# First layer's output product on one set of split weights, its norm's gain and bias folded into the next modulation, and two changes beside it

## The reference

```python
def _layer_norm(x, g, b):
    ...
    return ((xf - mu) * lax.rsqrt(var + EPS) * g + b).astype(x.dtype)

def _post_norm(x, y, gate, g, b):
    return _layer_norm(ALPHA * x + gate * y, g, b)

# layer ab (i = 0)
            h = x * (1.0 + sc[:, None]) + sh[:, None]
            y = _ab_mixer(h, ab_w_in[j], ab_pool_w[j], ab_pool_scale[j], ab_sgu_w[j], ab_sgu_b[j], ab_w_out[j])
            ...
                yc = _ab_mixer(hc, ab_w_in[j], ab_pool_w[j], ab_pool_scale[j], ab_sgu_w[j], ab_sgu_b[j], ab_w_out[j])
                ctx = _post_norm(ctx, yc, cgt, ab_ln_g[j], ab_ln_b[j])
            x = _post_norm(x, y, gt[:, None], ab_ln_g[j], ab_ln_b[j])
# layer cd (i = 1)
            hc = ctx * (1.0 + csc) + csh
            ... _split_cd(hc @ cd_w_in[j])
            h = x * (1.0 + sc[:, None]) + sh[:, None]
            f_in, f_gate, cq, ckv, kr, d_gate = _split_cd(h @ cd_w_in[j])
```

## Time and profile before

| | us |
|---|---|
| median of three runs | 3071.2 |
| lowest, highest | 3066.11, 3073.33 |
| profiled execution | 3069.66 |
| its span in the trace | 3067.8 |
| PE busy | 2848.2 (93%) |
| DVE, ACT, POOL busy | 1177.4, 971.5, 173.5 |
| mean DMA share of 16 engines | 25.3% |

### The profile page before, as it was taken

How to read it: one execution, slowest core, us unless ns; L and a number is a source line. 1 busy time by engine, 2 the same in 40 slices (tenths; PEclk the granted TensorE clock), 3 DMA queues, 4 the chain that set the end, 5 groups by cost and what they waited for, 6 DMA issues and landing times.

```text
span 3067.8 us, 33482 instructions
## 1 busy us (share of the span) xinstructions
PE 2848.2 (93%) x14067; PEld 2288.3 (75%) x14067; DVE 1177.4 (38%) x1720; ACT 971.5 (32%) x1437; POOL 173.5 (6%) x289
## 2 busy tenths in 40 slices
PE   4998949999799999899799999999998998899998
PEld 3876738667688888677488888888887775688887
DVE  2133472245533324344643332433324444543322
ACT  2211232244232223444432222322224445332221
POOL 0130010000100000000110000000000000000000
PEclk7999779999899999899699999999998998799999
DMA  7432123100223323211023323223232111123321
GB/s 249 145 102 83 55 82 109 48 1 1 76 96 96 96 96 96 59 56 45 24 70 110 99 95 122 83 96 96 96 110 73 55 42 42 42 92 95 103 100 72
DMA packets 208908, 253.89 MB, mean 83 GB/s; under 512 B 6384, under 2 KB 187191, under 8 KB 208760
## 3 DMA queue, kind: packets, MB, share of 16 engines
q1 hardware_dynamic: 208760, 251.76, 25.3%
HBM read 249.64 MB, written 2.10 MB: 82 GB/s over the span
## 4 chain that ended last, share of the span: by engine, by line
PE 85%; DVE 7%; ACT 3%; issue 2%; POOL 1%; SPq 1%; DMA 1%; DVEq 0%; POOLq 0%; ACTq 0%
PE psum L740 82%; DVE w_lo L1786 1%; PE psum L1199 1%; PE psum L810 1%; ACT w_hi L1357 1%; PE psum L1124 1%; POOL stats_first L2350 1%; DVE stats_first L1861 0%; DVE work L1854 0%; DVE X L1857 0%; DMA mod_w<-in_ab_w_mod 0%; SPq L713 0%; DVE h_lo L1795 0%; DVE spare_lo L1786 0%; SPq L618 0%
## 5 line engine op out<-in xcount | busy, mean ns | idle before, releaser
L740 PE MATMUL psum<-h_hi,w_hi 128*128 128x512 f32 (+1 forms) x2096 | 788.5, 376 | 34.9 <-issue 15.1
L740 PE MATMUL psum<-h_lo,w_hi 128*128 128x512 f32 (+1 forms) x2096 | 780.0, 372 | 0.0
L740 PE MATMUL psum<-h_hi,w_lo 128*128 128x512 f32 (+1 forms) x2096 | 779.6, 372 | 0.0
L1786 DVE TENSOR_TENSOR w_lo<-raw,w_hi 128x2048 fp32r<-128x2048 f32 (+1 forms) x182 | 419.0, 2304 | 806.3 <-ACT w_hi L1357 805.9
L740 PEld LDWEIGHTS psum<-h_hi,w_hi 128*128 128x128 f32 x2096 | 399.1, 190 | 111.1 <-issue 29.3
L740 PEld LDWEIGHTS psum<-h_hi,w_lo 128*128 128x128 f32 x2096 | 398.6, 190 | 68.5
L740 PEld LDWEIGHTS psum<-h_lo,w_hi 128*128 128x128 f32 x2096 | 399.0, 190 | 67.0 <-issue 1.0
L1357 ACT ACTIVATE w_hi<-raw 128x2048 fp32r<-128x2048 f32 (+1 forms) x182 | 344.0, 1893 | 240.0 <-PE psum L740 235.7
L740 PE MATMUL psum<-w_hi,ff_hi 128*128 128x512 f32 x576 | 226.5, 393 | 0.0
L740 PE MATMUL psum<-w_lo,ff_hi 128*128 128x512 f32 x576 | 226.4, 393 | 0.0
L740 PE MATMUL psum<-w_hi,ff_lo 128*128 128x512 f32 x576 | 223.9, 389 | 0.0
(11 more groups left out here) (282 smaller groups left out, 3371.7 us busy)
## 6 DMA issues: line engine op xcount, KB each, us to landing
raw<-in_ffn_w_gate SPq DMA_DIRECT2D x44, 1024.0 KB, 5.3
raw<-in_ffn_w_up SPq DMA_DIRECT2D x44, 1024.0 KB, 5.3
raw<-in_ffn_w_down SPq DMA_DIRECT2D x44, 1024.0 KB, 4.9
raw<-in_w_in SPq DMA_DIRECT2D x36, 512.0 KB, 5.1
raw<-in_ab_w_in SPq DMA_DIRECT2D x10, 1024.0 KB, 5.7
mod_w<-in_ab_w_mod SPq DMA_DIRECT2D x8, 1024.0 KB, 10.6
raw<-in_ab_w_out SPq DMA_DIRECT2D x8, 1024.0 KB, 4.9
raw<-in_w_out SPq DMA_DIRECT2D x8, 1024.0 KB, 4.9
```

The costliest lines, as they stand in the source:

```text
L740: return pe.matmul(o, lhsT, rhs, start=start, stop=stop, skip_group_check=True)
L1786: dve.tensor_tensor(lo[:, 0:nk * n], raw[c % 2][:, 0:nk * n], hi[:, 0:nk * n].bitcast(F32), ALU.subtract).then_inc(*w_lo_made.mark(key))
```

## The change

1. One set of split weights `ab_out` (four chunks, of which 2 and 3 lie in `ab_spare`) serves X and context. ACT and DVE split chunk 1 between the pool and the sgu part, chunks 2 and 3 after the last sgu head. `AB_TAIL` gives the order of norms and turns on ACT, DVE and POOL.
2. PE does chunks 0 and 1 for all X tiles, then chunks 2 and 3 tile by tile with the turns of X two behind; context chunks 0 and 1; then before each context tile's chunks 2 and 3 a turn of X. Layer cd's chunk 0 waits for X alone; the context turns stand behind its halves, and chunk 5 waits for context.
3. The norm's gain and bias go into the scale and shift of the next modulation (four small DVE operations; two more small loads at the start). X itself is needed later as residual and gets gain and bias from POOL, eight operations behind all six deviations. The gate diagonals no longer wait for them; layer cd's norm does.
4. DVE adds `sgu_b` (loaded to all partitions) in one operation more per sgu result; PE's 24 one-row products go.
5. DVE's half of a modulation is four `tensor_scalar` operations from PSUM with scale and shift.
6. Each step of a value product becomes two, of 64 query columns, on PSUM partitions 0 to 63 and 64 to 127.
7. The mixing constants have four semaphores. `band_bias`, `far`, `strict`, `tri` are issued after PE's last output tile of the FFN, the distances after its norm, the others after the fourth chunk. DVE's sums stand at chunk 3, ACT's exponential at chunk 4, the rest at chunk 5.

```diff
-    for part in ("ab_x", "ab_c"):
-        for c in range(4):
-            add((part, c), "ab_w_out", 0, "rows", 256 * c, 2, True)
+    for c in range(4):
+        add(("ab_out", c), "ab_w_out", 0, "rows", 256 * c, 2, True)
...
-        scale_odd = sb(ab_tail, "one_plus_scale_odd", [P, KT, 2])
+        ab_spare = [(sb(ab_tail, "spare_hi", [P, 2048], F32R), sb(ab_tail, "spare_lo", [P, 2048], F32R)) for _ in range(2)]
...
-                        landed = consts_landed[layer]
...
+                        raws_to(begin + 3)
+                        sp.wait_ge(*psum_full["y", before, NT - 1])
+                        sp.dma_start(band_bias[:, :, :], A["l_band_bias"][layer].rearrange("h q k -> q h k")).then_inc(*band_landed.mark(layer))
+                        sp.dma_start(far[:, :], A["l_far_bias"][layer].partition_broadcast(P)).then_inc(*band_landed.mark(layer))
+                        sp.dma_start(strict[:, :, :], A["k_strict"].rearrange("s p n -> p s n")).then_inc(*stick_landed.mark(layer))
+                        sp.dma_start(tri[:, :], A["k_tri"]).then_inc(*stick_landed.mark(layer))
+                        sp.wait_ge(*residual["normed", before, NT - 1])
+                        sp.dma_start(dist, A["k_distance"]).then_inc(*dist_landed.mark(layer))
+                        raws_to(begin + 4)
+                        sp.dma_start(sub_g[:, :], A["diff_subln_g_2"][layer].partition_broadcast(P)).then_inc(*lam_landed.mark(layer))
+                        for i, name in enumerate(("q1", "k1", "q2", "k2")):
+                            sp.dma_start(lam[:, i, :], A[f"diff_lambda_{name}_2"][layer].partition_broadcast(P)).then_inc(*lam_landed.mark(layer))
                         raws_to(CHUNK[s, 3])
...
-                        mm(bank(b, P, q * P), v_norm[:, off // P + q, hd * P:(hd + 1) * P], sgu_wT[:, hd, :], True, False)
-                        m = mm(bank(b, P, q * P), ones[0:1, :], sgu_b[0:1, hd * P:(hd + 1) * P], False, True)
+                        m = mm(bank(b, P, q * P), v_norm[:, off // P + q, hd * P:(hd + 1) * P], sgu_wT[:, hd, :], True, True)
                     done(m, ("sgu", hd, r))
...
+            def out_part(s, c, i, off):
+
...
+                for h in range(2):
+                    b = 2 * i + h
+                    if c == 0:
+                        claim(b, ("y", s, i, h))
+                    for kk in range(2):
+                        k = 2 * c + kk
+                        if s == "ab_x":
+                            ab_ready(i, k, h)
+                        m = mm3(bank(b), tokens(h_hi, k, off, P), tokens(h_lo, k, off, P), w[0][:, kk, h * BANK:(h + 1) * BANK],
+                                w[1][:, kk, h * BANK:(h + 1) * BANK], k == 0, k == KT - 1)
+                return m
+
+            def x_turn(i):
+                pe.wait_ge(*normed["ab_x", i])
                 turn("xo", i, X[:, i, :], (2 * i, 2 * i + 1))
 
...
+            def c_turn(i):
+                pe.wait_ge(*normed["ab_c", i])
+                turn("ct", i, CTX[:, i, :])
+
...
+            for c in range(2):
+                begin(("ab_out", c))
+                for i in range(NT):
+                    m = out_part("ab_x", c, i, i * P)
+                done(m, ("chunk", "ab_x", c))
+            for i in range(NT):
+                for c in (2, 3):
+                    if i == 0:
+                        begin(("ab_out", c))
+                    m = out_part("ab_x", c, i, i * P)
+                done(m, ("y", "ab_x", i))
+                if i > 1:
+                    x_turn(i - 2)
+            for c in range(2):
+                for i in range(NC):
+                    m = out_part("ab_c", c, i, L + i * P)
+                done(m, ("chunk", "ab_c", c))
+                end(("ab_out", c))
+            for i in range(NC):
+                x_turn(2 + i)
+                for c in (2, 3):
+                    m = out_part("ab_c", c, i, L + i * P)
+                done(m, ("y", "ab_c", i))
+            for c in (2, 3):
+                end(("ab_out", c))
+            rot.at = 0
...
-            pe.wait_ge(*h_lo_made["ct", NC - 1, 1])
+            pe.wait_ge(*h_lo_made["xo", NT - 1, 1])
...
+                if ch == 5:
+                    pe.wait_ge(*h_lo_made["ct", NC - 1, 1])
...
+                    if ch == 0:
+                        c_turn(j)
                     if ch == 1:
                         gate_row(("gate_cd", j))
...
                     for k in range(6):
-                        m = mm(bank(b, 64), probsT[(n - 2) % 2][:, k * P:(k + 1) * P], v_all[:, k, hd * 64:(hd + 1) * 64], k == 0, k == 5)
+                        for p0 in (0, 64):
+                            m = mm(psum[p0:p0 + 64, b * BANK:b * BANK + 64], probsT[(n - 2) % 2][:, k * P + p0:k * P + p0 + 64],
+                                   v_all[:, k, hd * 64:(hd + 1) * 64], k == 0, k == 5)
...
+                if s == "ab_out":
+                    act.wait_ge(*h_lo_made["sgu", 3, 1])
...
             for kind in ("pool", "sgu"):
+                if kind == "sgu":
+                    split_at(CHUNK["ab_out", 1])
...
+            split_at(CHUNK["ab_out", 2])
+            split_at(CHUNK["ab_out", 3])
+            for step, s, i in AB_TAIL:
+                if (step, s, i) == ("norm", "ab_c", 1):
+                    split_at(CHUNK["cd_in", 1])
...
                     if ch < 2:
                         copy(f_in[:, g, :], event, full(event), cd_kept)
+                        if ch == 0:
+                            turn("ct", j, h_hi, L + j * P, scale_odd[:, :, 1], shift_odd[:, :, 1])
...
-                act.wait_ge(*lam_made["sums", s])
-                act.activation(lam_s[:, 2:4], lam_s[:, 0:2], ACT.Exp).then_inc(*lam_exp.mark(s))
...
+                        if step[1] == 4:
+                            act.wait_ge(*lam_made["sums", s])
+                            act.activation(lam_s[:, 2:4], lam_s[:, 0:2], ACT.Exp).then_inc(*lam_exp.mark(s))
...
+                for k in range(4):
+                    m = dve.tensor_scalar(wv[:, k, :], full(event, P, k * P), scale[:, 4 + k:5 + k], shift[:, 4 + k:5 + k], ALU.mult, ALU.add)
+                m.then_inc(*part_made.mark(("sum", event)))
+                freed[event] = part_made["sum", event]
...
+                if s == "cd":
+                    dve.wait_ge(*ln_made["ab_x", t])
...
+            split_at(CHUNK["ab_out", 1])
...
-                    dve.tensor_tensor(w, full(event, n), u_gated[:, hd, off:off + n], ALU.mult).then_inc(*part_made.mark(event))
-                    freed[event] = part_made[event]
+                    dve.tensor_tensor(w.rearrange("p (q i) -> p q i", i=P), full(event, n).rearrange("p (q i) -> p q i", i=P),
+                                      sgu_b[:, hd, :].unsqueeze(1).broadcast_to([P, n // P, P]), ALU.add).then_inc(*part_made.mark(("biased", event)))
+                    freed[event] = part_made["biased", event]
+                    dve.wait_ge(*part_made["biased", event])
+                    dve.tensor_tensor(w, w, u_gated[:, hd, off:off + n], ALU.mult).then_inc(*part_made.mark(event))
                     split_lo_of(event, tokens(h_lo, 4 + hd, off, n), w, tokens(h_hi, 4 + hd, off, n))
...
+            dve.wait_ge(*scale_made["gain"])
+            dve.tensor_tensor(shift_odd[:, :, :], shift_odd[:, :, :], col("ab_ln_b", 0, 8).unsqueeze(2).broadcast_to([P, 8, 2]),
+                              ALU.mult).then_inc(*scale_made.mark("shift"))
+            dve.wait_ge(*scale_made["shift"])
+            dve.tensor_tensor(shift_odd[:, :, :], shift_odd[:, :, :], mod_cd[:, 0:8, :], ALU.add).then_inc(*scale_made.mark("cd"))
+            for step, s, i in AB_TAIL:
...
+                    if i == 2:
+                        split_at(CHUNK["cd_in", 0])
...
                 if ch == 1:
-                    dve.wait_ge(*ln_made["ab_x", NT - 1])
                     for j in range(2):
...
                     if kind == "chunk":
+                        if step[1] == 3:
+                            lambda_sums()
+                        if step[1] == 5:
+                            minus_lambda()
...
+            for step, s, t in AB_TAIL:
+                if step == "norm":
+                    ln_deviation(s, t)
...
             for t in range(NT):
-                layer_norm("ab_x", t, X[:, t, :], ab_b)
-            for t in range(NC):
-                layer_norm("ab_c", t, CTX[:, t, :], ab_b)
+                pool.wait_ge(*psum_full["xo", t, 1])
+                pool.tensor_tensor(X[:, t, :], X[:, t, :], ab_g[:, :], ALU.mult).then_inc(*ln_made.mark(("gain", t)))
+                pool.wait_ge(*ln_made["gain", t])
+                pool.tensor_tensor(X[:, t, :], X[:, t, :], ab_b[:, :], ALU.add).then_inc(*ln_made.mark(("ab_x", t)))
```

More of the change, by code:

```diff
@@ L396, in build @@
         scale1 = sb(first, "one_plus_scale", [P, KT, 2])
+        scale_odd, shift_odd = (sb(first, n, [P, KT, 2]) for n in ("one_plus_scale_odd", "shift_odd"))
         gate_rows = sb(first, "gate_rows", [P, 2, D])
```

(6 more changed lines are left out.)

230 lines of the change are left out of this document (74 added, 156 removed).

## The result

The changed kernel takes 2970.53 us in the median (2969.63 to 2971.69, 4 runs), against 3068.65 us (3062.01 to 3073.33, 4 runs) for the kernel before: a ratio of 0.968, 95% interval 0.966 to 0.970. The forecast was 2993 with a range of 2968 to 3035, so the time lies at the lower end of the range, and 98 us were gained where 78 were forecast.

The account below looks back on a forecast made before the run. PE was taken to bound the kernel, so edits pay where it stands still or has less to do. Tail −47, loads +0.6, constants −25, value products −6.5 sum to −78: 3071.2 to 2993 us, range 2968 to 3035.

Parts of the forecast that it names:

- The walk through the tail: First layer's output and start of `cd_in`: earlier starts and fewer stalls bring chunk 2 to 439, −47 us.
- the wait at the context turns: Context turns behind the halves of `cd_in` 0: the second waits 3.5 us for the norm of context tile 1.
- The term of the two loads: Start of the kernel: two more vector loads at the head of SP's queue cost +0.6 us, at most 2.4.
- The mixing constants: Starts of both mixing layers: PE's wait behind ACT's exponential goes, 12.5 us each, −25 us (−18 to −30).
- The residual wait: Start of each mixing layer: 1.6 us taken off 14.1, with ACT's split of chunk 2 late next.
- The value products: Attention and mixing: halves as column tiles overlap, −6.5 us in attention, 0 in mixing; ends −38 and +45.
- The passage between shapes: Around each attention group of value products: two passages into another shape cost 0.4 us, 0.2 each.
- The quarter of the groups: Attention: a quarter of the groups wait for ACT's probabilities anyhow, so −8 us becomes −6.5.
- rival 1: Value products: halves do not overlap, +45 us in place of −6.5, 3045 us; chance 0.12.
- Rivals 1 and 4: Value products: the fourth rival says each of 784 added records costs 0.108 us or more, 3102 us; chance 0.04.
- Rival 2: Value products: halves overlap and passages are free, −38 us, 2962 us; chance 0.08.
- Rival 3: Tail: DVE's diagonals and POOL's eight operations alternate, `cd_in` 1 waits 25 us, 3012 to 3030 us; chance 0.12.

Follow-up runs that it names:

- e4: The changed kernel with POOL's eight gain and bias operations on X made to wait for DVE's gate diagonals: 2958.91 us, ratio 0.964.
- e3: The changed kernel with value products whole and mixing constants as before: 3018.3 us, ratio 0.984.
- e8: The kernel before with only two more vector loads at the head of the load queue: one execution, 3059.58 us.
- e1: The kernel before with only the value products of attention and mixing split in two halves: 3040.98 us against 3065.09, ratio 0.991.
- e9: The kernel before with value products split in halves in the attention alone, mixing left whole: 3054.59 us against 3065.69, ratio 0.9961.

## Why the prediction was right, and where it was not

**What bounds the kernel** held: every part of the gain is PE starting earlier, standing still less or having less to do.

**The walk through the tail** held place by place, with one exception. Chunk 0 was forecast for 320.8 and came at 324.23; `cd_in` for 396.1 and came at 401.35; the wait for the diagonals for 7.6 us (5 to 15) and was 9.97. The exception is the wait at the context turns, forecast at 3.5 us and measured at 3.09: that these agree is luck. I had the second turn wait for the norm of context tile 1. That turn came at 419.63 and waited for nothing, as ACT had done the norm by 418.56. The 3.09 us stand inside the first turn and are for a bank, which the sum did not have. Chunk 2 came at 445.07 where 439 was forecast. Of the 6 us, 3.8 were there at 206 us already and came from the start; the tail itself gave −44.7 from there on, against −47. For the low clock behind the stalls the sum had about 6 us; behind the wait for the diagonals the traces of after and e4 put it at 2.2. e3 gives −46.8 by medians for tail and start together.

**The term of the two loads** was mis-sized: +0.6 forecast (at most 2.4), +3.5 at X's first transposes in the kernel after, +4.9 there and +4.5 at the output product in e8. I had priced the issue on SP and not what the modulation weights behind them lose; PE's waits for them are 0.98 us a chunk, instead of some 0.7, in both e8 and the kernel after, and the wait for the last ones ends 3.4 and 3.7 us later.

**The mixing constants** held: −25 forecast, −20.8 measured alone (by its interval −17 to −35 us), −13.7 and −13.4 us in the two starts of the kernel after, where 12.5 each was the forecast. The residual wait that I took off, 1.6 us a layer, did not show.

**The value products** were the step that failed in size: −6.5 forecast, −24.1 measured (e1). Three parts of that step were wrong. The passage between shapes costs 0.1 us a side, not 0.2, since I took it from products of one row of weights, which were another case than products of all rows with fewer columns. The quarter of the groups that I took as waiting for ACT was too much: in e9's trace the groups are shorter by 0.35 us or more, all but one, and of their 12.1 us in sum 9.7 arrive at the end of the attention. And mixing, which I put at 0, gave about 13 us by the difference of e1 and e9, which is loose. The mechanism was right: neighbouring column tiles run side by side, as in `mod_product`. But I took 0.09 us a record there for a price of each, beside 0.107 us of streaming. Its records start 0.007 us apart, three to a pass, and a pass recurs every 0.216 us, which is what one unsplit fp32 record with 256 moving columns takes alone. So the overlap was complete in that row already. The Trainium skill ("TensorE: Matmul & The Clock Gate", Part 3, on what overlaps) says that a weight load overlaps matmuls in flight only if the row group differs, and the prediction took from it that halves would win nothing (rival 1, 3045). The traces do not agree. In the kernel before a load of 128 columns on the same rows lasts 0.192 us by its record and recurs every 0.112; in the kernel after the load at 636.405 runs 0.138 us beside the product that started at 636.403. The rule speaks of loads; that two halves win nothing was my inference from it, and e1 refutes that.

**The rivals.** Rivals 1 and 4 are out by e1. Rival 2 (2962) was nearer in time than the forecast's centre, for a reason that it named in part: passages are cheap, though not free, and the halves gave 24 us and not its 38. Rival 3 named the right mechanism in the right place, but `cd_in` 1 waited 9.97 us, not the 25 of the rival and not the 7.6 of the sum. Its sign came true all the same: DVE's diagonals started at 430.92, past the 430 that I had named. e4 shows that the wait was avoidable.

## What to carry to other kernels

Fold an operation out of a critical path only together with a place for the work it leaves behind: here the gain and bias of X, which DVE needed at 738.8 and not before, ran from 414.9 on, on POOL, and held back the engine that was now critical; one wait gave back some 13 to 15 us. A product with few moving columns and 128 stationary ones is worth splitting in two column tiles on one PSUM bank, as a step then lasted half as long; four tiles gave nothing more, and by the estimate above the moving columns set that limit. Price a passage or a wait from a row of the same shape, and check small loads at the head of a queue by what stands behind them.

## What the runs showed of the hardware

- Two column tiles of 64 start 0.006 us apart, a pair recurs in 0.058 us, where one record of 128 weight columns with 64 moving recurs in 0.112. Four tiles of 32 take as long as the two (48 records in 0.88 us, 24 in 0.92).
- At full clock unsplit fp32 records recur by their moving columns: 0.429 us for 512, 0.216 for 256, 0.109 for 128. With 128 weight columns and two moving ones a record still recurs in 0.112 us.
- The granted clock differs between executions of the same instructions: 0.87 and 0.89 over a mixing layer of 1325 products, 307.0 and 300.2 us long.
- The DVE operations seen here that read and write SBUF alone wait for a running POOL operation, and POOL for them; those that read PSUM do not: 4.22 us against 1.30 for two splits, 1.35 against 1.36 for four modulation operations beside POOL and without it.
- With two more small loads at the head of the queue, the last modulation weights landed 3.4 to 3.7 us later (44.68 and 44.99 against 41.26).
